# Moving one fp32 spreading product behind the third forward group of a long convolution

## What is computed

```python
def diff_out(o, subln_g, lam_init):
    o = rmsnorm(o, subln_g) * (1.0 - lam_init)          # over the 128 channels of a head
...
def long_conv(z, k_f):
    L = z.shape[1]
    zf = jnp.fft.rfft(z.astype(F32), n=2 * L, axis=1)
    y = jnp.fft.irfft(zf * k_f[None], n=2 * L, axis=1)[:, :L]
    return y.astype(z.dtype)

def hyena_mixer(proj, p, k_f):
    ...
    for n, gate in enumerate((x1, x2)):
        z = gate * (long_conv(z, k_f[:, n]) + p["hy_skip"][n] * z)
    return rmsnorm(z, p["hy_norm"])
```

## Time and profile before

| what | value |
|---|---|
| median of three runs | 1491.4 us (1490.19 to 1491.43) |
| the profiled execution | 1489.46 us, span 1487.7 us |
| TensorE busy | 1454.1 us, 98% of the span |
| VectorE, ScalarE, GpSimd busy | 828.6, 622.1 and 317.5 us |
| mean granted TensorE clock | 0.998 of 2.4 GHz |
| the stretch of the change | 985 to 1010 us of the span |

### The profile page before, as it was taken

How to read it: one execution, slowest core, us unless ns; L and a number is a source line. 1 busy time by engine, 2 the same in 40 slices (tenths; PEclk the granted TensorE clock), 3 DMA queues, 4 the chain that set the end, 5 groups by cost and what they waited for, 6 DMA issues and landing times.

```text
span 1487.7 us, 17780 instructions
## 1 busy us (share of the span) xinstructions
PE 1454.1 (98%) x6972; PEld 1187.1 (80%) x6972; DVE 828.6 (56%) x1258; ACT 622.1 (42%) x1004; POOL 317.5 (21%) x301
## 2 busy tenths in 40 slices
PE   6999999999999999999999999999999999999998
PEld 5776768888878888888887878877788888888887
DVE  6455666544476643554457447777857544345434
ACT  5535773223453321344345336564435333123332
POOL 0263221011032200121015412126631111111102
PEclk9999999999999999999999999999999999999999
DMA  7452105654264544365326211224513233323321
GB/s 252 130 164 63 58 29 183 228 171 149 105 219 147 174 147 162 124 205 185 122 100 244 71 59 55 73 100 141 201 68 128 95 103 100 98 87 100 99 85 57
DMA packets 54174, 188.97 MB, mean 127 GB/s; under 512 B 6279, under 2 KB 7208, under 8 KB 53962
## 3 DMA queue, kind: packets, MB, share of 16 engines
q1 hardware_dynamic: 48010, 166.07, 33.7%
q0 software_dynamic: 4880, 17.30, 3.5%
q10 hardware_dynamic: 1200, 4.46, 0.8%
HBM read 175.21 MB, written 12.59 MB: 126 GB/s over the span
## 4 chain that ended last, share of the span: by engine, by line
PE 88%; DVE 4%; ACT 4%; issue 1%; POOL 1%; DMA 0%; ACTq 0%; SPq 0%; DVEq 0%
PE PS L470 87%; PE PS L483 2%; ACT TMP L1253 1%; ACT TMP L1251 1%; DVE wl L1778 1%; POOL wl L2486 1%; DVE TMP L2289 1%; ACT wh L1156 0%; DVE TMP L1828 0%; ACT TMP L1266 0%; ACT HTh L1177 0%; DVE HTl L2372 0%; DMA cst<-in_cst 0%; ACT TMP L1683 0%; ACT HTh L1676 0%
## 5 line engine op out<-in xcount | busy, mean ns | idle before, releaser
L1778 DVE TENSOR_TENSOR wl<-raw,wh 128x1024 fp32r<-128x1024 f32 x210 | 273.5, 1306 | 320.0 <-ACT wh L1156 319.6
L470 PE MATMUL PS<-HTh,wh 128*128 128x512 f32 (+1 forms) x1072 | 419.0, 391 | 4.0 <-DVE wl L1778 2.4
L470 PE MATMUL PS<-HTl,wh 128*128 128x512 f32 (+1 forms) x1072 | 413.8, 386 | 0.0
L470 PE MATMUL PS<-HTh,wl 128*128 128x512 f32 (+1 forms) x1072 | 411.9, 386 | 0.0
L1156 ACT ACTIVATE wh<-raw 128x1024 fp32r<-128x1024 f32 x228 | 239.2, 1053 | 275.0 <-PE PS L470 268.0
L470 PEld LDWEIGHTS PS<-HTh,wh 128*128 128x128 f32 x1072 | 201.4, 188 | 51.7 <-issue 10.1
L470 PEld LDWEIGHTS PS<-HTh,wl 128*128 128x128 f32 x1072 | 200.4, 188 | 41.5
L470 PEld LDWEIGHTS PS<-HTl,wh 128*128 128x128 f32 x1072 | 201.6, 188 | 38.7 <-issue 0.5
L470 PE MATMUL PS<-wh,FFh 128*128 128x512 f32 (+1 forms) x442 | 170.2, 385 | 0.0
L470 PE MATMUL PS<-wh,FFl 128*128 128x512 f32 (+1 forms) x442 | 169.9, 384 | 0.0
L470 PE MATMUL PS<-wl,FFh 128*128 128x512 f32 (+1 forms) x442 | 169.9, 384 | 0.0
(11 more groups left out here) (339 smaller groups left out, 2103.4 us busy)
## 6 DMA issues: line engine op xcount, KB each, us to landing
raw<-in_ws SPq DMA_DIRECT2D x268, 512.0 KB, 3.8
taps<-TMP SPq DMA_DIRECT2D x16, 256.0 KB, 2.5
tab<-in_spec POOLq DMA_DIRECT2D x8, 512.0 KB, 5.3
raw<-taps SPq DMA_DIRECT2D x8, 512.0 KB, 3.7
kd<-TMP POOLq DMA_DIRECT2D x16, 256.0 KB, 6.4
wh<-in_wd POOLq DMA_DIRECT2D x8, 512.0 KB, 4.0
wl<-in_wd POOLq DMA_DIRECT2D x8, 512.0 KB, 4.8
kf<-kd SPq DMA_DIRECT2D x8, 512.0 KB, 3.9
```

What stands on the lines that cost most here:

```text
L470: return nc.tensor.matmul(out, l, r, start=start, stop=stop, skip_group_check=True)
L1778: tt(WL[k][:, :n], RAW[RAW_AT["unit", u, 0] % RAWS][:, :n], f32(WH[k][:, :n]), ALU.subtract).then_inc(sem("lo_dve"), 1)
```

## The change

In the first convolution (`o == 0`) the first spreading product, `sub_scale(0)`, is issued behind `forward(0, 2)` and no longer behind `forward(0, 1)`. What follows from it is put one quarter later too: VectorE's `sub_high(0)`, ScalarE's `sub_high(0)` and `sub_diag(1)`, GpSimd's `sub_low(0)`. In the second convolution both expressions give the quarters they gave before (`2 - 2 * o` and `1 - o` are 0, `2 - o` is 1). No instruction is added or removed, and no tile or bank changes.

```diff
@@ -1042,7 +1042,7 @@
                     forward(o, f)
                     if f == 0 and o == 0:
                         sub_sums()
-                    if f == 1 - o:
+                    if f == 2 - 2 * o:
                         sub_scale(3 * o)
                     if f == 3 and o == 0:
                         sub_scale(1)
@@ -1619,7 +1619,7 @@
                         act(SUBR[:, 16:32], SUBR[:, 16:32], ACT.Sqrt, scale=2.0 ** -8,
                             bias=1e-6 * 2.0 ** -8).then_inc(sem("sub_rt"), 1)
                         sub_diag(0)
-                    if f == 1:
+                    if f == 2 - o:
                         sub_high(3 * o)
                         if o == 0:
                             sub_diag(1)
```

## The result

| | median | runs | ratio, 95% interval |
|---|---|---|---|
| kernel before | 1490.2 us | 22 | |
| changed kernel | 1492.37 us (1490.75 to 1496.02) | 22 | 1.0015 (1.0009 to 1.0022) |
| changed kernel, a second series | 1492.84 us (before there 1491.27) | 12 | 1.0013 (1.0004 to 1.0022) |

The kernel became 0.15% slower, 2.2 us by the ratio (1.3 to 3.3). The interval lies above 1, so the slowing is real, and it is on the side that was forecast, if under the 3.0 us from which the prediction would have called it slower. 1492.9 us was predicted. Its profiled execution took 1491.97 us, with a span of 1490.2.

The account below looks back on a forecast made before the run. TensorE, busy 1454.1 of 1487.7 us, was taken as the bound. 1.41 us gained against 2.79 lost and a 0.10 restart gave +1.5 on 1489.46, 1490.9; the median's 1.9 more made 1492.9, 8 in 10 within 1489.9 to 1495.0.

Parts of the forecast that it names:

- The gain: TensorE, first backward group: starts at 1001.94 instead of 1003.35 as the wait for the first diagonal goes, 1.41 us gained.
- The new wait: TensorE, first backward group, three products before its end: a wait of 2.4 to 2.8 us for bank 5, released by L2276.
- the walk through VectorE: VectorE from 1002.14: third spectral product follows the second without idling, then L2276 ends at 1006.69, or 1006.42 without a hold.
- the hold by GpSimd's L2655: VectorE's L2291, third spectral product: held by GpSimd running until 1004.93, so it ends at 1005.49 instead of 1005.22.
- The sum: Whole kernel: 1.41 us gained and 2.79 lost, the restart 0.10 more, giving +1.5 us, bounds +1.1 and +2.1.
- its own range: Time of the likeliest case, from its bounds and the 1.2 us spread of three runs: 1491.6 to 1494.1 us.
- What is queued behind: Next diagonal on ScalarE, GpSimd's low half, fourth spectral product: none costs; the diagonal has 1.6 us left before TensorE asks.
- Rival (a): Clock falls to half rate in TensorE's new idle time, 1.7 us more: +3.2 us, 1494.6 us; chance 0.17.
- (b): Bank 5 is free in time, L2276 done before 1004, so the wait only vanishes: 1490.0 us; chance 0.07.
- (c): A further wait, for a diagonal or weight split later than walked: 2 to 4 us more, 1494 to 1497; chance 0.06.

Follow-up runs that it names:

- pe_only: Against the kernel before, only TensorE's first spreading product moved behind the third forward group, its readers left in place: ratio 0.9992, run again 0.9989.
- ring_bank: Changed kernel with the first spreading product in a bank of the forward groups' ring of four, so no accumulator waits for it: ratio 0.9997 against the kernel before.
- readers_late: Kernel before with only the spreading product's readers on VectorE, ScalarE and GpSimd one quarter later, TensorE's order as before: ratio 1.0025.
- bank4: Changed kernel with the first spreading product in bank 4, which is accumulator 2's: ratio 1.0028 against the kernel before, seven runs.
- longer: Changed kernel with VectorE's L2276 product written twice more ahead of the one that frees the bank: ratio 1.0035 against the kernel before, five runs.
- filled: Changed kernel with nine more unread 128x512 products on TensorE ahead of accumulator 3's wait: ratio 1.0013, the changed kernel beside it 1.0013.
- gap_sq: Kernel before with 30 shorter waits in the first FFN product, each group waiting until VectorE has squared the group before: 1548.55 us.

## Why the prediction came out right, step by step

- **The gain.** Forecast 1.41 us at the fourth accumulator. In the trace its turn comes 0.23 us behind 1005.17, 13.64 us behind S, where it was 14.97 before: 1.33 gained. Right, and pe_only, which keeps the gain alone, was measured 1.2 and 1.6 us faster. One step towards it doesn't follow from its row: that the third group's weights and banks were there before 998.5, since the group ran without a wait only from 1000.2 on in the trace of before. The changed kernel's trace shows that nothing held it.
- **The new wait.** Forecast 2.4 to 2.8 us, released by L2276; measured 2.17, 2.35 and 2.49. Mechanism right, size 0.1 to 0.4 too large. Two terms of the walk through VectorE were off and nearly cancel. L2289 doesn't follow L2293 after 0.60 but after 0.81 us (1002.57 to 1003.38), because it also waits until the previous spectral product is finished. And the hold by GpSimd's L2655, forecast at 0.27, was 0.02, since L2291 came later to it: L2655 ended at 1005.94 and L2291 at 1006.48, 0.54 behind, so the rule read from the earlier trace rows held and only had nothing to hold. What is left is the start of the second spectral product: 7.81 us behind S, right behind the factors, instead of 8.12 (998.54 - 990.42) in the trace that I started from, since the half rate came 0.5 us later in this execution and caught TensorE less before its second group's end. In the other two profiles it starts 7.94 and 8.11 us behind S, and their waits are longer in the same order, 2.35 and 2.49.
- **The sum.** +1.5 us; local distances +1.15, +1.29 and +1.42. That the absolute time came so near (1492.9 against 1492.37) is luck in part: the forecast started from the median of three runs, 1491.4, where 22 runs have 1490.2, and its +1.5 was 0.7 under the 2.2 of the ratio, so two errors of opposite sign all but cancel. The lower end of its own range, 1491.6, doesn't come out of the terms that it names: 1491.4 + 1.1 less half or all of the 1.2 us of spread is 1491.9 or 1491.3.
- **What is queued behind.** No wait at the second spreading product, as forecast, with 1.8 us left where 1.6 were forecast (the diagonal is done at 1009.52, the product starts at 1011.28). The slack was real and small: ring_bank used it up and waited 0.87.
- **Rival (a), the fall in the wait,** got only 0.17, mainly on the strength of one row, the 2.37 us at 15.60 that no fall followed. That reading failed: after the same wait the clock fell in the changed kernel's own trace at 17.0, and after 2.1 us it fell in 16 of 30. One occurrence of a wait without a fall says little here. Nor was the fall at 994.77 an instance of an idle TensorE: it came behind one-column products during which the engine is shown as busy. In the three profiles of the changed kernel it didn't occur at this wait, in readers_late (2.34), bank4 (2.93) and longer (3.96) it did. How often it happens in the changed kernel stays open.
- **Rivals (b) and (c)** didn't occur in the changed kernel; (b) is what pe_only makes, and (c) what ring_bank ran into.
- **What the sum left out.** The timed ratio says 2.2 us (1.3 to 3.3), the profiles 1.15 to 1.42, so what is left over is small beside the interval and may be chance. The second stretch at half rate, hidden in part by the old wait and by nothing in the new order, adds about 1.0 in the executions that have it (four of the thirteen profiles, counting all kernels), by estimate some 0.3 on the mean. Falls in the new wait may add the rest; that isn't shown. How the remaining half microsecond divides is open: filled and the changed kernel could not be told apart by their times.

## What to carry to other kernels

Before a product is moved to hide its input's wait, look up who reads its output bank and who wants that bank next: a wait of 1.2 us went, one of 2.2 to 2.5 us came, because the reader was moved with it behind six instructions of its engine. Moving TensorE's product and leaving the reader in place gave the gain. A wait on the path may also be hiding something (here a second stretch at half rate, and near 17 us a whole one), and a profile with one occurrence of it tells neither how often the clock falls nor what it costs. Count over many waits, and measure by a distance between two instructions near the place, not by the span.

## What the runs showed of the hardware

- A stretch at half rate behind a wait or behind the one-column products lasted 3.41 to 3.42 us in every trace, or twice that. In one series each, after idle times of 2.07 to 2.22 us in an otherwise busy TensorE it came in 16 of 30 cases, after 1.41 to 1.69 us in 0 of 28, after a single one of 2.21 us it didn't. After 2.93, 3.06 and 3.96 us it came in 3 of 3. The shortest idle time with a fall was 1.90 us (`longer`, at 17.64). The Trainium skill (TensorE: Matmul & The Clock Gate, Part 1) says of a kernel's start that the number of matmuls at the low clock differs from run to run of the same kernel. The traces agree in that the clock's changes vary between executions: 15.60 and 16.89 are the same wait without and with a fall.
- A stretch at half rate need not cost time: behind 16.89 it cost about nothing, since waits of 1.21 and 0.46 us were gone behind it; the second one in gap_sq cost 0.84 us where an unhidden one costs 1.7.
- Sixteen one-column products (32 records, 3.63 us at full rate) were followed by one stretch in eight profiles, two in four and none in one, although the engine is shown as busy during them.
